# Order of the expert rounds: two fixed rounds first, then overflow and fixed in turn, two overflow rounds last

## What is computed

```python
h = silu(einsum('nd,edh->neh', xt, w_gate)) * einsum('nd,edh->neh', xt, w_up)
y = einsum('neh,ehd->nd', h * gates[:, :, None], w_down)
```

## Time and profile before

| | us |
|---|---|
| three runs | 1618.97, 1625.09 (median), 1628.69 |
| the profiled execution | 1634.04 |
| its span | 1632.0 |
| rounds of layer 0, first gate and up product to the last down product | 515.9 to 716.1 |
| rounds of layer 1, the same | 1386.5 to 1591.2 |

### The profile page before, as it was taken

The page is one execution under the profiler, slowest core; times in us unless marked ns, Lnnn a source line. Parts: engine busy times, 40 slices in busy tenths (PEclk is TensorE's granted clock), DMA queues, the critical chain, the costliest instruction groups (busy, mean ns, idle before and its releaser), DMA issues.

```text
span 1632.0 us, 21643 instructions
## 1 busy us (share of the span) xinstructions
PE 1487.7 (91%) x8511; PEld 987.5 (61%) x8511; DVE 518.3 (32%) x1075; ACT 370.2 (23%) x854; POOL 203.3 (12%) x241
## 2 busy tenths in 40 slices
PE   7999999998998999998999989989998984989990
PEld 6888888874775333357888864448874673323330
DVE  1421144413264111124433334442513165111115
ACT  0111110223042111114100047650224023111113
POOL 0000000000002332221410000000000001344323
PEclk9999899999998999999999999989999995989995
DMA  7211331543566999875458687932435235989836
GB/s 297 79 52 55 105 127 52 206 180 130 206 243 229 357 398 383 318 307 210 151 201 334 234 340 289 340 139 118 181 104 206 104 139 212 364 343 392 343 129 170
DMA packets 84909, 357.73 MB, mean 219 GB/s; under 512 B 21834, under 2 KB 25450, under 8 KB 58178
## 3 DMA queue, kind: packets, MB, share of 16 engines
q1 hardware_dynamic: 50336, 271.23, 43.5%
q0 software_dynamic: 23584, 48.03, 8.7%
q10 hardware_dynamic: 10889, 37.10, 5.8%
HBM read 403.97 MB, written 33.11 MB: 268 GB/s over the span
## 4 chain that ended last, share of the span: by engine, by line
PE 79%; DVE 6%; DMA 6%; ACT 5%; issue 3%; POOL 1%; POOLq 0%; ACTq 0%; SPq 0%; DVEq 0%
PE PS L625 75%; DMA MKV<-in_moe_w_gu,OVR 3%; PE PS L1180 2%; DMA W<-y_rows,SLOT 1%; DVE EX L1261 1%; DMA O<-in_moe_w_down,OVR 1%; PE PS L706 1%; DVE SM L1318 1%; PE PS L957 1%; ACT BIG L2143 1%; PE PS L1041 1%; ACT TOK L2085 1%; ACT BIG L2148 1%; ACT TOK L2091 1%; ACT X L1928 0%
## 5 line engine op out<-in xcount | busy, mean ns | idle before, releaser
L625 PE MATMUL PS<-X,W 128*128 128x260 f32 x1264 | 290.4, 386 | 13.3 <-DMA W<-in_ab_w_in 9.1
L625 PEld LDWEIGHTS PS<-X,W 128*128 128x128 f32 x1264 | 240.1, 191 | 53.5 <-issue 12.6
L625 PE MATMUL PS<-O,W 128*128 128x260 f32 x1024 | 230.6, 386 | 2.4 <-DVE O L1638 1.6
L625 PEld LDWEIGHTS PS<-O,W 128*128 128x128 f32 x1024 | 195.0, 191 | 37.6 <-issue 3.4
L1866 ACT ACTIVATE BIG<-PS 128x512 f32<-128x512 f32 (+2 forms) x161 | 75.1, 466 | 303.5 <-PE PS L625 209.2
L625 PE MATMUL PS<-W,BIG 128*64 128x512 f32 x512 | 117.1, 611 | 2.0 <-DVE BIG L1766 2.0
L2362 POOL TENSOR_TENSOR SM<-SM,O 128x5 f32<-128x5 f32 x2 | 0.4, 196 | 833.6 <-DVE SM L1716 833.6
L1771 DVE SCALAR_TENSOR_TENSOR BIG<-BIG,SM,PS 128x256 f32<-128x256 f32 x32 | 15.4, 480 | 250.4 <-ACT BIG L2217 250.4
L625 PE MATMUL PS<-MKV,BIG 128*64 128x512 f32 (+1 forms) x384 | 90.9, 523 | 1.0 <-ACT BIG L1866 1.0
L625 PEld LDWEIGHTS PS<-W,BIG 128*64 128x64 f32 x512 | 36.8, 141 | 71.4 <-issue 71.4
L625 PE MATMUL PS<-W,TMP 128*16 128x512 f32 (+2 forms) x512 | 76.5, 556 | 0.0
(11 more groups left out here) (326 smaller groups left out, 1856.4 us busy)
## 6 DMA issues: line engine op xcount, KB each, us to landing
W<-in_moe_w_gu SPq DMA_DIRECT2D x64, 1024.0 KB, 10.4
TMP<-in_moe_w_down SPq DMA_DIRECT2D x32, 1024.0 KB, 10.2
W<-in_fox_kt SPq DMA_DIRECT2D x64, 512.0 KB, 5.7
W<-in_fox_v SPq DMA_DIRECT2D x64, 512.0 KB, 6.3
W<-in_mem_kt SPq DMA_DIRECT2D x16, 1024.0 KB, 9.0
W<-in_cache_mem_v SPq DMA_DIRECT2D x16, 1024.0 KB, 8.1
y_rows<-BIG ACTq DMA_DIRECT2D x32, 512.0 KB, 9.0
W<-in_mem_wkv SPq DMA_DIRECT2D x13, 1024.0 KB, 4.9
```

The lines of the kernel that those rows point to most:

```text
L625: return nc.tensor.matmul(out, lhsT, rhs, start=start, stop=stop, **kw)
```

## The change

Only the order of the rounds is changed. In the order before, each fixed round is followed by an overflow round. In the new one fixed rounds 0 and 1 run one behind the other, then overflow 8, fixed 2, overflow 9 and so on to overflow 13, fixed 7, and then overflow 14 and overflow 15 run one behind the other. Every wait that looks up a place in ROUNDS moves with it.

```diff
-ROUNDS = (0, 8, 1, 9, 2, 10, 3, 11, 4, 12, 5, 13, 6, 14, 7, 15)
+ROUNDS = (0, 1, 8, 2, 9, 3, 10, 4, 11, 5, 12, 6, 13, 7, 14, 15)
```

## The result

The changed kernel takes 1659.68 us (median of 4 runs, 1654.34 to 1667.72) against 1624.15 before: ratio 1.0224, 95% interval 1.0171 to 1.0277, so 35.5 us slower. The direction was forecast, the size was not: the forecast was +21, its range ended at 1658.0. The profiled execution has a span of 1652.4 us.

A forecast was written before the change was run, and what follows sets the result against it. The prediction took the rounds to be bound by TensorE's products, so order matters only through waits. Terms -1.7 + 1.6 + 5.4 + 15.9 = +21 us gave 1655 against the profiled execution, 1646 against the median; range 1633 to 1658.

The forecast's parts named there:

- the mechanism of the end: Last two overflow rounds share buffers, so TensorE waits for the last weights: 15.9 us in layer 0, 5.4 in layer 1.
- the start: Place 1 of each layer: TensorE waits 0.8 us for fixed_dn(1), 1.6 us together; nothing won at the first overflow set.
- The middle of a stage: the same distances: Places 2 to 13: loads keep their distances from asking to need, so waits stay; 0 but for 1.7 us saved.
- -1.7 for layer 0: Place 13 of layer 0: the wait of 1.7 us goes, as the last fixed gate and up set has landed earlier.
- Rival (a): Middle of layer 1: SP's queue 2 to 4 MB fuller at three real overflow sets; +28 us, 1653, chance 0.22.
- the end of layer 1: Last overflow set, moving nothing: waits of 1.9 and 2.5 us plus 1 for a slow clock, 5.4; bounds 4.4 and 9.1.
- The term of the last down product: Layer 1, last down product: it waits 2.5 us for overflow_dn(7), which is asked for only when down(14) ends.
- the end of layer 0: Last overflow set, two real loads: wait 6.8, slow clock 3.0, down product 6.1, together 15.9 us; bounds 6.4 and 18.7.
- my bound of 9.8: Layer 0, place 15: longest landing time in us allowed for the last overflow gate and up load, taken as 7.0.
- a sign of being wrong: End of layer 0: kv1 loads still landing when overflow_gu(7) is asked for would mean more cost there; no size given.
- the term of the down product: Layer 0, last overflow down product: 14.4 us from end of down(14) to end of down(15) against 8.2, so 6.1 more.
- The base: Whole kernel: the profiled execution lies 9 us above the median of the runs, 1625.1, so 1655 becomes 1646.

The follow-up runs named there:

- ScalarE's load one place later: Order of the kernel before, with only ScalarE's load into TMP for the next product issued one place later: 1622.93 us, ratio 0.9998 to before.

## Why the prediction was right or wrong

**Right: the direction and the mechanism of the end.** Two overflow rounds side by side share one set of buffers, and the 17 us of cover become 5.0 and 1.75. Removing the last set gives 26 us back in the medians and 23.6 by stage; the prediction had 21.3 for the ends.

**Right: the start.** 0.63 and 0.62 us for fixed_dn(1) against 0.8, and nothing won at the first overflow round.

**Wrong, and the step that failed: "The middle of a stage: the same distances", -1.7 for layer 0 and 0 for layer 1 in the sum.** The runs showed +5.9 and -1.4. I argued from phases: each queue is asked for the same things in the same distances, 12 us later. That is true of the askings and not of what has landed. The DMA engines were at share 1.01, so what counts is the bytes due ahead of an overflow set, and these grew by one fixed set (6 MB) where the time grew by one place (12 us). Layer 0 went from 2.4 to 8.3 us of waits and slow products. Rival (a) had this mechanism, but for layer 1 alone, where I saw three real overflow sets in a row. It came in layer 0, where the second set moves nothing and the third is real. In layer 1 there was a wait already, and it only moved, to place 4 where I had forecast place 6. The -1.7 had no ground either: it was the wait of 1.72 us, which an execution with the old order there can also be without. 2 MB fewer removed the wait of layer 0, and 2 MB more made it in the old order; this is shown by runs and not only argued. Why layer 1's wait kept its size is not shown.

**Wrong in size: the end of layer 1,** 5.4 predicted, 9.0 measured, the upper bound (9.1). The last empty load took 1590.01 - 1586.68 = 3.3 us instead of 2.1, and both waits, though 3.05 and 3.87 us only, had a slow product behind them (1.7 each), of which I had counted 1 in all. The term of the last down product was right: 3.87 - 1.31 = 2.6 against 2.5.

**Wrong in size, and partly by luck near: the end of layer 0,** 15.9 predicted, 17.4 measured. The last load took 10.9 us and not 7.0, over my bound of 9.8. Two loads beside it had been misjudged: kv1's (1.2 MB still to land, which the prediction had named as a sign of being wrong), and ScalarE's load into TMP. I had noted that ScalarE's wait for fixed round 7 goes, and not that its load goes forward with it. Against that the slow product cost 1.8 and not 3.0, and the term of the down product was 5.05 and not 6.1, since its second load landed in 725.71 - 720.34 = 5.4 us and not 6.8.

**The base.** To take off the 9 us between the profiled execution and the median was right, but not all of them lay outside the rounds. Against the profiled execution of "ScalarE's load one place later" (1623.08 us), before was 2.4 us longer ahead of the rounds and 4.1 between them, and also 2.7 and 1.4 in the rounds of the two layers. Measured from that execution, the rounds of after are 26.8 + 9.8 = 36.6 us longer, and the medians differ by 36.8. So the 32.2 of the sum is low by some 3 us, most likely because before's execution had small waits of its own.

## What to carry to other kernels

When a change of order keeps every distance between asking and need, add up the bytes due by each point as well, and the time there is for them: with the DMA engines full, more bytes than the time holds are a wait there, even if they were asked for 20 us earlier. Holding a load back or changing who goes first then only renamed the wait here, or made it longer; of what was tried only fewer bytes removed it. And where a round uses a single set of buffers, two such rounds side by side pay the whole way from release to landing, with whatever other loads the same change brings forward to that moment.

## What the runs showed of the hardware

**What an indirect load costs that moves nothing.** POOL's queue moved 0.00 MB for the last sets of layer 1, and still the four loads were issued 1.3 us apart, and TensorE waited 3.05 us for the last of them.

**How little idle time brings a slow product.** After 3.05 us of waiting in layer 1 the granted clock was 0.67 over the next row of 16 matmuls, and in layer 0, behind 10.59 us, 0.66 (columns as in the earlier trace rows):

```profile
705.90:711.30 5.40, 5.36 (x18) 1.74 (x20) 0.00 (x0) 0.00 (x0) 0.00 (x0) 0.66 0.00 0
1590.00:1595.20 5.20, 5.20 (x18) 1.62 (x20) 0.00 (x0) 0.00 (x0) 0.00 (x0) 0.67 0.00 0
```

Three times the wait gave the same 1.7 to 1.8 us of loss. Behind 5.66 us in the middle of layer 0 it was 2.67. So the loss isn't in proportion to the wait. Nor does the wait alone decide whether there is one. Six executions have the changed order's wait before place 15 of layer 1, of 2.7 to 3.05 us; behind it the row took 5.35 us in five of them and 3.65 in one, the second of these two (fixed_dn behind the overflow set in the changed order). The last down product of layer 0 took 5.35 us in before, behind idle times of 1.39 and 1.05 us, and 3.65 behind the same two in the order of before with 2 MB more, the first of these two:

```profile
714.26 3.65 PE L631 MATMUL PS<-O,BIG 128*64 128x512 f32 x16 [1.05 <-DMA O<-in_moe_w_down,OVR]
1598.80 3.65 PE L627 MATMUL PS<-X,BIG 128*64 128x512 f32 x16 [3.04 <-DMA MKV<-in_moe_w_gu,OVR]
```

A wait of 3 us thus cost nearly 5 in most executions, and 3 in one.

**The same instructions, 9 us apart.** The stretch before the rounds took 513.0 us in the profile of before and 504.3 in that of after, and from 504 to 513 in the others. Most of it arises between 150 and 200 us, with TensorE busy throughout: up to 150 us the two executions had got through 694 and 697 matmuls, up to 200 us through 957 and 991. Before:

```profile
150.00:200.00 50.00, 50.00 (x265) 44.25 (x264) 7.43 (x15) 6.61 (x16) 0.00 (x0) 0.80 0.30 108
```

After, the same 50 us:

```profile
150.00:200.00 50.00, 50.00 (x296) 44.50 (x295) 12.93 (x21) 8.16 (x20) 0.00 (x0) 0.93 0.35 129
```

A mean of 0.80 is 20 of the 50 us at the lower level of 1.2 GHz, one of 0.93 is 7 us; the execution with less of it got through more products. Why it was granted differently for the same work stays open. It is a reason to compare stages and not spans here.
